# A two-block network: four modulation matrices of the second block move from the first mixer to the second, and are summed on VectorE there

## The chip, the cores and the metric

The kernel runs as one program on one core of a Trainium2 chip. The metric is the device time of a run in microseconds, the median of three runs. The core has five engines with an instruction stream each: TensorE (PE in the profile, with its weight loads as PEld), VectorE (DVE), ScalarE (ACT), GpSimd (POOL) and SyncE (SP), which here only issues DMAs. The streams meet in semaphores: an instruction adds to one, another stream waits until it has reached a number.

## What is computed

A sequence of 256 rows of 1024 features in fp32 goes through two transformer blocks. Each block takes a condition vector c and makes six modulation vectors of it, each of them the product of silu(c) with a matrix of 1024 x 1024 (4 MB):

```python
# first block: six parts mx[0..5], and mc[0..1] for 256 context rows
mx = split(silu(c) @ w_ada + b_ada, 6)
hx = rms_norm(x, g_pre_mix) * (1 + mx[1]) + mx[0]
x = x + mx[2] * rms_norm(token_mixer(hx, hc, ...), g_post_mix)      # mLSTM heads and a convolution
hx = rms_norm(x, g_pre_ffn) * (1 + mx[4]) + mx[3]
x = x + mx[5] * rms_norm(moe_ffn(hx, ...), g_post_ffn)              # 64 experts, top 8, one shared

# second block
shift1, scale1, gate1, shift2, scale2, gate2 = split(silu(c_2) @ w_ada_2 + b_ada_2, 6)
h = rms_norm(x, norm1_g) * (1 + scale1) + shift1
proj = h @ w_in                                                     # q, k, v, u, two branch gates
mixed = (g_attn * y_attn + g_pool * y_pool) @ w_out
x = x + gate1 * mixed
h2 = rms_norm(x, norm2_g) * (1 + scale2) + shift2
x = x + gate2 * hier_moe(h2, ...)                                   # 32 experts, top 2 of one group
return rms_norm(x, norm_f_g)
```

In the kernel's names the matrices are ada0 to ada5 for the first block and adb0 to adb5 for the second. adb0 and adb1 are shift1 and scale1; the four of the change are adb2 (gate1), adb3 (shift2), adb4 (scale2) and adb5 (gate2). None of these four is needed before the second mixer's end.

## The kernel before, in words

The work has four stages: first mixer (0 to about 256 us), first expert layer (to 754), second mixer (to about 965), second expert layer (to the end).

**Weights of the first mixer** come through three buffers of 4 MB, `BUF[0]` to `BUF[2]`, in the order of the list `STREAM` (name, buffer) at line 115. SyncE loads an item as soon as PE has counted the buffer's item before it as used (`stream_used`, in the order `USED`; `stream` at L543). After the sixteen items SyncE goes on with the pieces of the expert layer (1 MB each, `load_piece` at L603): those in `BUF[0]`, `BUF[1]` and `BUF[2]` wait for adb4, adb5 and w_out to be used up, those elsewhere for more. From the third group of experts on they also wait for `order_known`, which the routing gives.

**A modulation product** is `ada_parts` (L1055): silu(c) is the stationary side with 32 columns, the matrix the moving side of 512 columns; four products run side by side in the array and leave four partial sums for each vector in PS[5] and PS[6], which gather all vectors as rows. VectorE adds the bias (`ada_sum`, L1822) into `ada_rows`. Of these rows PE makes columns over the 128 partitions (`column_sums`, L1070) and, for the gates, one row spread over all partitions (`gate_rows`, L1076); `mixer_gate` (L2135) multiplies these with a gain.

**First mixer, PE from L1231.** For j = 0, 1, 2 the state products (L1240) are made, with the first sum over the convolution's channels (L1247) after j = 0 and adb0 and adb1 after j = 0 and 1. Then come the scores `qk` (L1257), the second sum of the convolution (L1262, for the variance) and the first two `seen_largest` (L1266, a product that spreads a row of maxima). Then the four heads' directions, gi = 0 to 3: one of adb2 to adb5, a wait for VectorE's last result (`hm_ready`), eight pairs of small products (L1287, L1288; called a head below), a further `seen_largest`. After that the output product (`mixed_out`, L1295) of the convolution's half, column sums (two banks of 30 columns) and gate rows, four transposes a block, the other half of the output product, and further gate rows between it and the transposes for the routing.

**VectorE beside it (L2018 to L2100)**: `states`, the convolution's mean and variance, `seen` (L2046), `convolution_normalised` (L2038) after the first score, and for each head the scaling and sum that read the four banks (L2071, L2075), a denominator and the normalised rows. **ScalarE** (L837 to L870) copies qk (L845), takes the root of the variance, the exponentials and, between the second and third of them, the four Silus of the convolution (L856); another kind of function than the last one costs a table load.

**Second mixer, PE from L1617**: transposes, then the projections in items of `ITEMS2` (q and k at L1627, v and u at L1637, the branch gates at L1667 in four pairs between the attention's heads), tables and pool products (L1643 to L1657), attention, the branch product (L1727), the output product (L1742), routing. SyncE loads the six items through `BUF[0]` and `BUF[1]` in turn (L660 to L675), then the second layer's expert pieces (L690 on).

## Time and profile before

| | |
|---|---|
| median of 3 runs | 1431.79 us (1428.27 to 1434.04) |
| profiled execution | 1431.23 us, its span 1429.5 us |
| mean granted clock of PE | 0.919 |
| busy: PE, DVE, ACT, POOL | 1177.6, 364.9, 181.8, 89.6 us |
| instructions | 21079 |
| HBM | 505.34 MB read, 354 GB/s over the span |

A timeline shows start and duration of instructions (one fp32 matrix product is two records, so "x32" are 16 products), and in brackets the idle time of the engine just before and what ended it. The chain that ended last is followed back from the last instruction to what released each step. The DMA share is the mean over the core's 16 DMA engines.

### The profile page before, as it was taken

Reading aid. Unit: us, or ns where it says so; the run is one execution under the profiler, and the core shown is the slowest. Engines: PE = TensorE matmul, PEld = TensorE weight load, DVE = VectorE, ACT = ScalarE, POOL = GpSimd, SP = SyncE. Lnnn points to the kernel's source line nnn. Section 1 sums busy time; section 2 is a strip of 40 time slices with the busy share of each in tenths; the row PEclk is TensorE's granted clock in tenths of the full one; section 3 lists DMA queues with packets and bytes.
Section 4 is the critical chain, followed back from the end, with each engine's and each line's share of the span. In section 5 each row is a group of like instructions: output and inputs, shape, how many; then the busy total and the mean of one; then the engine's idle time right before and its main releaser. Section 6 shows DMA issues by size and latency. Waiting matters only on the chain.

```text
span 1429.5 us, 21079 instructions
## 1 busy us (share of the span) xinstructions
PE 1177.6 (82%) x8938; PEld 607.4 (42%) x8938; DVE 364.9 (26%) x941; ACT 181.8 (13%) x370; POOL 89.6 (6%) x118
## 2 busy tenths in 40 slices
PE   5999989999999989999987999898475564655647
PEld 3663435655555545455546554344121221212212
DVE  1598755511111111111103054334010100100002
ACT  1210112411111111111113012012000000000000
POOL 2498000000000000000000000000000000000000
PEclk9999999999999999999998999999777886877878
DMA  9965993789999999999994222839999999999995
GB/s 388 344 262 236 422 420 146 304 321 388 419 420 420 420 420 420 420 420 420 420 429 191 118 118 118 368 130 382 428 428 428 426 428 429 427 429 425 430 424 222
DMA packets 51802, 507.81 MB, mean 355 GB/s; under 512 B 6445, under 2 KB 7637, under 8 KB 11001
## 3 DMA queue, kind: packets, MB, share of 16 engines
q1 hardware_dynamic: 49689, 503.07, 84.6%
q10 hardware_dynamic: 2016, 3.36, 0.7%
q8 instruction: 72, 1.18, 0.3%
q14 instruction: 25, 0.20, 0.0%
HBM read 505.34 MB, written 1.06 MB: 354 GB/s over the span
## 4 chain that ended last, share of the span: by engine, by line
PE 48%; DMA 26%; SPq 14%; DVE 7%; issue 3%; ACT 1%; POOL 1%; DVEq 0%; POOLq 0%; ACTq 0%
SPq L628 11%; DMA W<-in_w_expert_gate 6%; PE PS L1774 6%; PE PS L1598 5%; DMA W<-in_w_expert_up 4%; PE PS L1667 4%; PE PS L1608 3%; SPq L626 3%; PE PS L1788 3%; PE PS L1063 3%; PE PS L1464 3%; PE PS L1438 2%; DMA scr<-in_w_expert_up 2%; DMA W<-in_w_expert_down 2%; DMA hx<-in_w_expert_up 2%
## 5 line engine op out<-in xcount | busy, mean ns | idle before, releaser
L1774 PE MATMUL PS<-W,scr 128*32 128x512 f32 x640 | 143.6, 719 | 85.5 <-DMA W<-in_w_expert_gate 20.5
L1774 PE MATMUL PS<-scr 128*32 128x512 f32 x288 | 109.2, 724 | 62.7 <-DMA W<-in_w_expert_gate 31.8
L2299 DVE TENSOR_TENSOR scr<-scr,PS 128x256 f32<-128x256 f32 (+1 forms) x33 | 23.4, 710 | 518.3 <-PE PS L1774 262.9
L1598 PE MATMUL PS<-W,scr 128*32 128x256 f32 (+1 forms) x1936 | 136.4, 388 | 10.0 <-DMA W<-in_we_up 8.3
L1464 PE MATMUL PS<-scr 128*128 128x512 f32 x248 | 114.7, 605 | 0.0
L1598 PEld LDWEIGHTS PS<-W,scr 128*32 128x32 f32 (+1 forms) x1936 | 78.8, 116 | 67.4 <-issue 16.8
L1774 PEld LDWEIGHTS PS<-W,scr 128*32 128x32 f32 x640 | 34.7, 129 | 148.5 <-issue 103.3
L1438 PE MATMUL PS<-scr 128*128 128x128 bf16 x1536 | 91.8, 220 | 0.0
L908 ACT COPY scr<-PS 128x512 f32<-128x512 f32 x66 | 38.5, 585 | 410.1 <-PE PS L1438 407.4
L1438 PEld LDWEIGHTS PS<-scr 128*128 128x128 bf16 x1536 | 89.4, 98 | 1.0 <-issue 0.6
L1788 PE MATMUL PS<-W,scr 128*32 128x512 f32 x288 | 65.8, 678 | 16.4 <-DMA scr<-in_w_expert_down 7.6
L1464 PEld LDWEIGHTS PS<-scr 128*128 128x128 f32 x248 | 44.6, 189 | 60.1 <-issue 60.1
L1774 PEld LDWEIGHTS PS<-scr 128*32 128x32 f32 x288 | 25.1, 130 | 104.5 <-issue 70.9
L1788 PE MATMUL PS<-scr 128*32 128x512 f32 x176 | 57.0, 669 | 8.6 <-DMA W<-in_w_expert_down 7.6
L1598 PE MATMUL PS<-scr 128*32 128x256 f32 (+1 forms) x592 | 56.2, 387 | 6.8 <-DMA hx<-in_we_up 4.3
L1774 PE MATMUL PS<-hx,scr 128*32 128x512 f32 x96 | 56.8, 758 | 0.0
L1667 PE MATMUL PS<-W,hx 128*128 128x512 f32 x128 | 56.0, 595 | 0.0
L1608 PE MATMUL PS<-W,scr 128*32 128x512 f32 (+1 forms) x416 | 54.7, 596 | 0.0
L913 ACT ACTIVATE scr<-PS 128x256 f32<-128x256 f32 (+1 forms) x33 | 14.4, 435 | 300.4 <-PE PS L1774 226.6
L1063 PE MATMUL PS<-W,sc 128*32 128x512 f32 x384 | 48.0, 644 | 3.0 <-DMA W<-in_w_ada 2.9
L775 POOL TENSOR_SCALAR_AFFINE_SELECT W<-W 128x2048 f32<-128x2048 f32 x1 | 1.9, 1950 | 683.9 <-DVE W L2409 683.9
L770 POOL TENSOR_SCALAR scr<-scr,convw 128x256 f32<-128x256 f32 x44 | 44.5, 1010 | 4.3
(430 smaller groups left out, 1463.6 us busy)
## 6 DMA issues: line engine op xcount, KB each, us to landing
W<-in_we_up SPq DMA_DIRECT2D x46, 1024.0 KB, 24.6
W<-in_we_gate SPq DMA_DIRECT2D x45, 1024.0 KB, 24.4
W<-in_w_ada SPq DMA_DIRECT2D x10, 4096.0 KB, 15.0
W<-in_w_expert_gate SPq DMA_DIRECT2D x20, 2048.0 KB, 29.8
W<-in_w_expert_up SPq DMA_DIRECT2D x20, 2048.0 KB, 29.6
W<-in_we_down SPq DMA_DIRECT2D x38, 1024.0 KB, 24.6
W<-in_w_expert_down SPq DMA_DIRECT2D x16, 2048.0 KB, 32.3
scr<-in_w_expert_gate SPq DMA_DIRECT2D x10, 2048.0 KB, 26.9
```

The source lines that it names most:

```text
L626: expert = at if at < STATIC1 else sp.value_load(order[0:1, at:at + 1], min_val=1, max_val=E1) - 1
L628: sp.dma_start(piece_view(piece), src).then_inc(S[f"ring{SETS1.index(piece[0:2]) % 12}"], 16)
L770: step(g.tensor_scalar(tmp, upad[:, i, :, j:j + ROW], convw[:, 4 * j + i:4 * j + i + 1], None, ALU.mult))
L908: a.copy(hTe[:, 4 * q:4 * q + 4, :], PS[4 + q][:].rearrange("p (k s) -> p k s", k=4)).then_inc(S["x_hTe"], 1)
L1063: last = mm(PS[5 + h][32 * j:32 * j + 32, :], sc[:, 2 * j + kk, 30 - row:62 - row], ada_columns(n, 2 * j + kk, h), start=(row == 0 and kk ...
L1438: last = mm(PS[4 + k // 4][:, (k % 4) * P:(k % 4 + 1) * P], hs[:, part, b, k * P:(k + 1) * P], Sb[:, b, :], start=(q == 0), stop=(q == NB ...
L1464: last = mm(PS[2 * b + h][:, :], Ct[:, b * P:(b + 1) * P], Y[:, h * 512:(h + 1) * 512], start=False, stop=False)
L1598: m = mm(PS[4 + kind][at:at + size, 0:F1], hTe[:, k, at:at + size], piece_view((g, kind, j))[:, k, :], start=(k == 0), stop=(k == KD - 1))
L1608: m = mm(PS[6 + h][at:at + size, :], aT[:, c, at:at + size], piece_view((g, 2, j))[:, c, h * 512:(h + 1) * 512], start=(c == 0), stop=(c = ...
L1667: last = mm(PS[6 + n % 2][:, :], hT[:, k, b * P:(b + 1) * P], w2k[2 + half][:, k, h * 512:(h + 1) * 512], start=(k == 0), stop=(k == KD - 1))
L1774: m = mm(PS[4 + kind][j * CAP2:(j + 1) * CAP2, :], hTe[:, k, j * CAP2:(j + 1) * CAP2], piece_view2((g, kind, j))[:, k, :], start=(k == 0), ...
L1788: m = mm(PS[6 + h][j * CAP2:(j + 1) * CAP2, :], aT[:, c, j * CAP2:(j + 1) * CAP2], piece_view2((g, 2, j))[:, c, h * 512:(h + 1) * 512], st ...
```

## The change

1. `STREAM` ends with adb0, w_out, adb1; adb2 to adb5 are no longer in it. The buffers are dealt anew, w_out is loaded whole into `BUF[2]` (before, three of its eight parts lay in scratch), and the rows `post_mix` and `post_ffn` are loaded by SyncE ahead of in_qkv, into places of their own.
2. In the first mixer, PE's second sum of the convolution stands between the state products of j = 1 and adb1. The head loop has no modulation product; behind each head (`behind_head`) stand the next `seen_largest`, the gate rows and the column sums of the remaining vectors (18 columns, one bank). A head waits for `out_taken` (VectorE has read its banks) where it waited for `hm_ready`. VectorE takes the variance ahead of `states(2)`, normalises the convolution and adds the modulation's bias ahead of the heads, and makes the gates in the loop. ScalarE runs the Silus ahead of the copies of qk.
3. The four matrices come in the second mixer: SyncE's `late_modulation`, ahead of the third projection item, loads four bias tiles (128 x 1024, row 0 holding the bias) and 16 parts of 1 MB through three slots. VectorE adds each part with two fused multiply-adds of 1024 columns (`late_part`), in between its copies of q, k, v and u. PE sums over the partitions: the gates by a product with ones (four of 512 columns, behind the pool's first products), shift and scale by `late_columns`, 16 products with one moving column, after the attention. ScalarE copies the results (`second_gates` ahead of the exponentials of the attention).
4. The second block's normalised rows are transposed in the other order of features (`every_kd`), and w_in_2 and its gain are laid out to match; the products are the same in number and size.

```diff
-STREAM = [("ada0", 0), ("ada1", 1), ("in_conv", 2), ("in_og", 0), ("in_qkv", 1), ("ada2", 2), ("ada3", 0), ("ada4", 2), ("ada5", 0),
-          ("adb0", 2), ("adb1", 0), ("adb2", 1), ("adb3", 2), ("adb4", 0), ("adb5", 1), ("w_out", 2)]
-USED = ["ada0", "ada1", "in_conv", "in_og", "ada2", "ada3", "ada4", "ada5", "in_qkv",
-        "adb0", "adb1", "adb2", "adb3", "adb4", "adb5", "w_out"]
+STREAM = [("ada0", 2), ("ada1", 1), ("in_conv", 0), ("in_og", 2), ("in_qkv", 1), ("ada2", 0), ("ada3", 2), ("ada4", 0), ("ada5", 2),
+          ("adb0", 0), ("w_out", 2), ("adb1", 1)]
+USED = ["ada0", "ada1", "in_conv", "in_og", "ada2", "ada3", "ada4", "ada5", "in_qkv", "adb0", "adb1", "w_out"]
 AT = {n: i for i, n in enumerate(USED)}
-AHEAD = 5
+
+
+ADA_LATE = [("adb3", "shift"), ("adb4", "scale"), ("adb2", "gate"), ("adb5", "gate")]
+PARTS, PART_K, PART_SLOTS, PART_WORDS = 4, 2, 3, 2048
+FREE_RING = (8, 9, 10)
...
+            for name, src in (("post_mix", A["g_post_mix"][0]), ("post_ffn", A["g_post_ffn"][0])):
+                row(rowd[name], src)
             for n, _ in STREAM[4:]:
...
+                    sp.wait_ge(S["ada_summed"], 5)
+                    sp.wait_ge(S["gates_made"], 2)
...
+                    sp.wait_ge(S["stream_used"], AT[("adb0", "adb1", "w_out")[place // 4]] + 1)
...
+            def late_modulation():
+
+                sp.wait_ge(S["y_done"], 4)
+                for m, (n, _) in enumerate(ADA_LATE):
+                    sp.dma_start(late_sums[n], A["ada_bias_late"][m]).then_inc(S["ring4"], 16)
+                for i in range(len(ADA_LATE) * PARTS):
+                    if i >= PART_SLOTS:
+                        sp.wait_ge(S["part_used"], i - PART_SLOTS + 1)
+                    sp.dma_start(part_slots[i % PART_SLOTS], A["w_ada_late"][i // PARTS, i % PARTS])\
+                        .then_inc(S[f"ring{FREE_RING[i % PART_SLOTS]}"], 16)
+
             for n, i in AT2.items():
+                if i == 2:
+                    late_modulation()
...
+            sp.wait_ge(S["ada_summed"], 10)
             fill((5, 4, 6, 7))
...
+            act.wait_ge(S["norm_ms"], 3)
+            step(a.activation(crstd, crstd, ACT.Sqrt), S["norm_root"])
+            act.wait_ge(S["cn_ready"], 1)
+            for i in range(4):
+                step(a.activation(mixT[:, 4 + i, :], ctmp[:, i, :], ACT.Silu, scale=cols[:, C_LNG + i:C_LNG + i + 1],
+                                  bias=cols[:, C_LNB + i:C_LNB + i + 1]), S["mixT_conv"], wait=False)
             act.wait_ge(S["qk_mm"], 2)
             for r in range(2):
                 step(a.copy(qk.rearrange("p c (q r) t -> p c q r t", r=2)[:, :, :, r, :],
                             PS[r][:].rearrange("p (c q t) -> p c q t", c=2, q=2)), S["qk_ready"], wait=False)
 
-            act.wait_ge(S["norm_ms"], 3)
-            step(a.activation(crstd, crstd, ACT.Sqrt), S["norm_root"])
             for gi in range(4):
                 act.wait_ge(S["exp_in"], gi + 5)
                 step(a.activation(dts[gi % 2], dts[gi % 2], ACT.Exp, scale=-1.0), S["exp_out"])
-                if gi == 1:
-                    for i in range(4):
-                        act.wait_ge(S["cn_ready"], 1)
-                        step(a.activation(mixT[:, 4 + i, :], ctmp[:, i, :], ACT.Silu, scale=cols[:, C_LNG + i:C_LNG + i + 1],
-                                          bias=cols[:, C_LNB + i:C_LNB + i + 1]), S["mixT_conv"], wait=False)
-
+
+            act.wait_ge(S["ada_summed"], 5)
+            for n, (i, b, s) in enumerate(((4, 1, 0), (1, 0, 2))):
+                mod_columns(5, i, b, s, n == 1)
+            root_table()
...
+            def second_gates():
+
+                for n in range(4):
+                    act.wait_ge(S["ada_summed"], 6 + n)
+                    step(a.copy(gate2[:, n // 2, n % 2 * 512:n % 2 * 512 + 512], PS[n][:]), S["ada_ready"], wait=False)
...
+            act.wait_ge(S["ada_summed"], 10)
+            step(a.copy(modc[:, 1, 2:4, :, 2], PS[3][:, 384:400].rearrange("p (m k) -> p m k", m=2)), S["ada_ready"], wait=False)
...
+                elif j == 1:
+                    pe.wait_ge(S["csq_ready"], 1)
+                    conv_sum(7)
                 if j < 2:
...
-            for gi, n in enumerate(("adb2", "adb3", "adb4", "adb5")):
+            def behind_head(gi):
+
+                if gi < 2:
+                    seen_largest(gi + 2)
+                if gi == 0:
+                    pe.wait_ge(S["ada_rows_ready"], 3)
+                    pe.wait_ge(S["gate_sel"], 2)
+                    gate_rows(0, (5, 6))
+                elif gi == 1:
+                    pe.wait_ge(S["gates_made"], 1)
+                    gate_rows(1, (5, 6))
+                elif gi == 2:
+                    pe.wait_ge(S["gates_made"], 2)
+                    column_sums(5, N_ADA1, every_kd(ada_rows)).then_inc(S["ada_summed"], 1)
+
+            for gi in range(4):
                 c, d = gi // 2, gi % 2
-                ada_parts(n)
                 pe.wait_ge(S["sT_ready"], gi + 1)
                 if gi:
-                    pe.wait_ge(S["hm_ready"], gi)
+                    pe.wait_ge(S["out_taken"], gi)
                 else:
 
                     pe.wait_ge(S["norm_ms"], 3)
@@ -1288,8 +1323,7 @@
                     last = mm(PS[(3, 7)[h % 2]][:, hp * 129:hp * 129 + 129], qT[half, hp, c * P:(c + 1) * P],
                               state[half, 0 if c == d else 1, d, hp, :], start=True, stop=True)
                 last.then_inc(S["out_mm"], 1)
-                if gi < 2:
-                    seen_largest(gi + 2)
+                behind_head(gi)
...
-            pe.wait_ge(S["ada_rows_ready"], 3)
-            column_sums(4, 30, ada_rows.rearrange("t (k p) -> t k p", k=KD))
-            column_sums(7, 30, every_kd(ada_rows)).then_inc(S["ada_summed"], 1)
-            pe.wait_ge(S["gate_sel"], 4)
-            gate_rows(0, (5, 6))
...
+            for n in range(4):
+                if n % 2 == 0:
+                    pe.wait_ge(S["ada_rows_ready"], 3 + (3, 4)[n // 2])
+                mm(PS[n][:, :], ones[:], gate2[:, n // 2, n % 2 * 512:n % 2 * 512 + 512], start=True, stop=True).then_inc(S["ada_summed"], 1)
...
+            pe.wait_ge(S["ada_ready"], 7)
+
+            def late_columns():
+
+                for m, n in enumerate(("adb3", "adb4")):
+                    for k in range(KD):
+                        at = 384 + KD * m + k
+                        last = mm(PS[3][:, at:at + 1], every_kd(late_sums[n])[:, k, :], ones[:, 0:1], start=True, stop=True, skip_group_check=True)
+                last.then_inc(S["ada_summed"], 1)
...
+            late_columns()
 
 
             loaded2(4)
             pe.wait_ge(S["attn_done"], 1)
...
-            states(2)
             dve.wait_ge(S["conv_sum_mm"], 2)
             step(v.tensor_scalar(crstd, PS[7][:, 0:T], 1.0 / CONV_C, EPS, ALU.mult, ALU.add), S["norm_ms"])
+            states(2)
...
+            def scored(gi):
+
+                dve.wait_ge(S["exp_out"], gi + 5)
+                dve.wait_ge(S["qk_ready"], 2)
+                step(v.tensor_tensor(dts[gi % 2], dts[gi % 2], qk[:, gi // 2, :, :], ALU.mult), S["sT_ready"])
+
+            convolution_normalised()
+            dve.wait_ge(S["stream_used"], AT["adb1"] + 1)
+            for h in range(2):
+                ada_sum(1, h, S["ada_rows_ready"] if h else None)
             dve.wait_ge(S["exp_out"], 4)
             seen(0)
+            seen(1)
+            scored(0)
+            scored(1)
             for gi in range(4):
...
+                    step(v.tensor_tensor(rows, rows, nd[:, :, 0:DV], ALU.add))
+                if gi < 2:
+                    scored(gi + 2)
+                    mixer_gate(gi, 3 + gi)
...
+            def late_part(i):
+
+                n = ADA_LATE[i // PARTS][0]
+                if i == 0:
+                    dve.wait_ge(S["ring4"], 16 * RING_USES[4] + 16 * len(ADA_LATE))
+                ring = FREE_RING[i % PART_SLOTS]
+                dve.wait_ge(S[f"ring{ring}"], 16 * RING_USES[ring] + 16 * (i // PART_SLOTS + 1))
+                for k in range(PART_K):
+                    kk = i % PARTS * PART_K + k
+                    step(v.scalar_tensor_tensor(out=late_sums[n], in0=part_slots[i % PART_SLOTS][:, k * D:(k + 1) * D], scalar=sc[:, kk, 32:33],
+                                                in1=late_sums[n], op0=ALU.mult, op1=ALU.add), S["part_used"] if k == PART_K - 1 else None)
+                if i % PARTS == PARTS - 1:
+                    dve.sem_inc(S["ada_rows_ready"], 1)
+
+            parts_before = (6, 9, 12, 15)
             for q in range(4):
+                for i in range(parts_before[q - 1] if q else 0, parts_before[q]):
+                    late_part(i)
                 dve.wait_ge(S["in2_mm"], q + 1) if q < 3 else dve.wait_ge(S["stream2_used"], 1)
                 dst = (qT2 if q < 2 else kT2)[:, 2 * (q % 2):2 * (q % 2) + 2, :]
                 step(v.tensor_copy(dst, PS[4 + q][:].rearrange("p (m t) -> p m t", m=2)), S["in2_ready"])
+            late_part(len(ADA_LATE) * PARTS - 1)
```

## Rows read from the trace of the kernel before

**Rows 1.** The page, share of each of 40 slices of 35.7 us: granted clock, DMA.

```profile
PEclk9999999999999999999998999999777886877878
...
DMA  9965993789999999999994222839999999999995
```

**Rows 2.** Timeline of PE, end of the first expert layer (start, duration, engine, line, what).

```profile
743.95 5.20 PE L1608 MATMUL PS<-scr 128*32 128x512 f32 x32 [2.41 <-DMA scr<-in_we_down]
```

**Rows 3.** Timeline of PE, first mixer from 160 to 252 us.

```profile
161.46 3.64 PE L1063 MATMUL PS<-W,sc 128*32 128x512 f32 x32
...
167.71 1.99 PE L1262 MATMUL PS<-scr,ones 128*128 128x256 f32 x8
...
174.92 0.49 PE L1287 MATMUL PS<-scr 128*128 128x129 f32 x2
...
178.26 1.12 PE L1268 MATMUL PS<-hx,ones 128*128 128x512 f32 x2
...
198.52 6.55 PE L1063 MATMUL PS<-W,sc 128*32 128x512 f32 x32 [2.10 <-DMA W<-in_w_ada]
...
247.38 3.60 PE L1079 MATMUL PS<-scr 128*128 128x512 f32 x8
```

**Rows 4.** Chain that ended last, first mixer (start, duration, piece).

```profile
208.41 13.93 PE PS L1300 x32
...
222.34 5.53 PE PS L1073 x32
...
227.87 3.58 PE PS L1079 x4
```

**Rows 5.** The load of adb2 issued at 153.1 us, and its time to landing.

```profile
L554 SPq DMA_DIRECT2D W<-in_w_ada x1: 327/327/327, 153.1 to 153.1; - x1
...
DMA to landing us min/median/max: 16.2/16.2/16.2
```

**Rows 6.** Timeline of DVE, first mixer.

```profile
168.12 0.43 DVE L2023 TENSOR_TENSOR scr<-scr 128x258 f32<-128x258 f32 x1
...
172.34 1.12 DVE L2052 SCALAR_TENSOR_TENSOR scr<-PS,small,scr 128x128 f32<-128x128 f32 x4
...
173.38 0.68 DVE L1925 TENSOR_TENSOR hx<-ident,small 128x512 f32<-128x512 f32 x1
...
174.69 1.75 DVE L2041 RECIPROCAL scr<-scr 128x256 f32<-128x256 f32 x1
...
176.48 1.22 DVE L2042 TENSOR_TENSOR scr<-scr 128x1024 f32<-128x1024 f32 x1
...
187.09 1.13 DVE L2071 TENSOR_SCALAR scr<-PS,small 128x129 f32<-128x129 f32 x4 [3.58 <-PE PS L1288]
...
188.25 0.89 DVE L2075 TENSOR_TENSOR scr<-scr,PS 128x129 f32<-128x129 f32 x4
```

**Rows 7.** Timeline of ACT, first mixer.

```profile
168.18 1.07 ACT L845 COPY hx<-PS 128x512 f32<-128x512 f32 x2 [25.96 <-PE PS L1257]
...
177.78 1.28 ACT L856 ACT_TABLE_LOAD   x1 [3.30 <-DVE scr L2042]
...
179.08 2.07 ACT L856 ACTIVATE scr<-scr,cols 128x256 f32<-128x256 f32 x4
```

**Rows 8.** Windows, first mixer: busy time of each engine, granted clock, DMA share, GB/s.

```profile
198.00:204.00 6.00, 5.48 (x28) 1.39 (x32) 2.47 (x8) 0.00 (x0) 0.00 (x0) 0.50 0.96 406
...
225.00:231.00 6.00, 6.00 (x16) 4.07 (x17) 0.00 (x0) 0.40 (x3) 0.00 (x0) 0.50 0.14 59
```

**Rows 9.** Chain, second expert layer: one matrix product with one moving column.

```profile
986.04 0.22 PE PS L1422 x2
```

**Rows 10.** Timeline of DVE: its last work before the second mixer's projections.

```profile
764.83 1.90 DVE L2184 TENSOR_SCALAR hx<-PS,am,modc 128x256 f32<-128x256 f32 x4 [0.65 <-PE PS L1330]
```

**Rows 11.** DVE line 2161, all of its instructions (ns minimum, median, maximum).

```profile
L2161 DVE SCALAR_TENSOR_TENSOR x<-hx,small,x x8: 750/752/752, 242.9 to 760.3; 128x512 f32<-128x512 f32 x8
```

**Rows 12.** The 1 MB load of x on an empty queue, to landing.

```profile
DMA to landing us min/median/max: 5.5/5.5/5.5
```

112 lines of the change are left out of this document (41 added, 71 removed).

## The prediction

> **What bounds the kernel now.** I read the slices of the page first. The DMA row [rows 1] is full in slices 9 to 20, the first expert layer, and from slice 27 on, the second one. It reads 2, 2, 2, 8, 3 in slices 22 to 26 (786 to 965 us), the second mixer, so 16.8 MB of weights find room there. In the first mixer (up to about 256 us) it is full only from 140 to 222 us, while four of the matrices in question arrive. Both expert layers end with the loads: the last down product of the first one still stands 2.41 us for its weights [rows 2]. But the loads of a layer start from events of the mixer before it (w_out used up, the routing known, the places of the ring free again). So each layer is shifted as a whole by what its mixer gains or loses, and the question is how long the two mixers' chains are.
>
> The timeline of PE in the first mixer comes next [rows 3]. From 153 to 208 us PE alternates between a modulation product (3.6 us a matrix, 16 products of which four run side by side) and a head (eight pairs of rows, 3.4 us). The products fill the time in which VectorE normalises the head before. Behind the heads the chain of waits has the first half of the output product, the column sums and a gate row [rows 4], and the second half ends where the next gate rows start, at 247.4 us [rows 3].
>
> **What goes.** Four products of 3.6 us, with the loads they stand for (the one at 198.52 took 6.55 us instead of 3.6: PE had stood 2.1 us for its load, and the granted clock was 0.50) [rows 3, 8]. Between the two halves of the output product 5.53 of column sums and 3.58 of gate row go [rows 4]. The gate rows and copies behind 247.4 run beside VectorE and ScalarE, which set the end there: I count them at nothing.
>
> **What the new order costs until head 0.** adb1 is now the third in the load queue, behind adb0 and the whole of w_out, as adb2 was behind adb0 and adb1. adb2's load, issued at 153.1, landed 16.2 us later [rows 5], at 169.3; issue and bytes ahead of it are the same for adb1 now. PE is through with the state products of j=1 at 161.5, where adb1's product began before, and with the moved sum for the convolution (1.92 more) at 163.45 [rows 3]. It stands 5.9 us.
> Then, at full clock: adb1's product 3.6 (172.9); state products and six VectorE steps of 0.46, as before 3.5 from the first product's start (176.4) [rows 6]; reciprocal 1.75 and product 1.22 (179.5) [rows 6]; ScalarE now runs the four Silus before the copies of qk, table load 1.28, Silu 2.07, copies 1.07 (184.0) [rows 7]; the first maximum 0.86 (184.9) [rows 3]; VectorE twice 1.12 and 0.68 before the first score, then 0.69 (189.2) [rows 6]; head 0, 3.36 (192.5). Before, head 0 ended at 178.3 [rows 3]: 14.2 us later.
>
> **The heads.** With the products gone they form a circle. After head 0: scaling 1.13 and sum 0.89 free the banks [rows 6], but PE has a maximum (some 0.9) and a gate row (1.79, half of the 3.60 for two) to do [rows 3], so head 1 ends 6.0 later. From then VectorE leads: per head 2.05 for the banks, 1.1 for the next `seen`, 0.6 for the denominator, 0.7 to 1.4 for the rows, 0.7 for the score and 1.4 for the gate, together 6.6 and 7.3; head 2 ends 6.3 after head 1, and head 3, which waits for the second gate and eight column sums (2.2, at 0.24 to 0.28 each), 7.5 after head 2, at 212.2 [rows 6]. That is 19.8 us for three heads where 30.1 stood (178.3 to 208.4).
> Output product 13.9, transposes and copies 2.0, output product 13.9 [rows 3, 4]: 242.1 us against 247.4, a gain of 5.3 at full clock.
>
> **The clock.** All this holds at full clock, and that is the doubt. After a stand of 2.1 us the granted clock was 0.50 from 198 to 204; in the column sums, with PE busy throughout but with 30 moving columns, it was 0.50 from 225 to 231 [rows 8]. The new order stands 5.9 us before adb1 and 8.4 us between qk and the first maximum, and has a third weak stretch from head 2 to the column sums. I charge: adb1's product 2.1 (between 0 and the 3.0 of the row 6.55 against 3.6); the maximum, head 0 and the gate row behind it 5.0 (0 to 6.0, all of them doubled); column sums, head 3 and the start of the output product 5.0 (0 to 6.5). Together 12.1, bounds 0 and 15.5. So the first mixer ends 6.8 us later than before; bounds 5.3 earlier and 10.2 later.
> The Trainium skill (TensorE: Matmul & The Clock Gate, Part 1) says that for modelling, the ramp penalty of a typical kernel is under 1% of its span, and advises against fitting it. Taken as leave to drop the term it gives the sum of the first rival below; taken as a ceiling, 14.3 us here, it leaves my charge standing. The row at 0.50 clock, 3.0 us lost on one product, speaks for charging each such stretch.
>
> **The second mixer.** The loads: 2.1 MB of bias rows and 16.8 MB of parts, from the end of the first expert layer, behind the projection weights that are still arriving; at 0.42 MB per us 45 us, in a stretch where the DMA row reads 2. VectorE: 32 fused multiply-adds on 1024 columns. The trace has 512 columns at 0.752 us [rows 11] and none at 1024; twice that is the upper bound (1.50), the lower is the 1.22 of a plain product of that width [rows 6]; I take 1.32 with its gap, as part of the 0.752 is fixed. A part takes 2.64, sixteen 42. A slot turns around in 2.64, some 0.5 of issue and at most the 5.5 us of a 1 MB load on an empty queue [rows 12]: 8.6 over three slots, 2.9 a part; the loads alone need 2.5. VectorE is free at 766.7 [rows 10]; bias rows and first part, 3.1 MB or 7.4 us, come behind what is still arriving then, so the start is about 773. From there sixteen parts at 2.7 to 2.9 with four copies of 0.7, partly in the gaps, end at 819 to 822. PE wants these copies at 821.8, after 56 us of projections that need nothing of VectorE. I charge 0.5; bounds 0, and 8 if a part takes 3.5. Up to 3.2 a part the projection weights issued behind the late loads also come in time. If this cover went, each 0.1 us a part would cost 1.6.
> PE gets four products of ones with the gate sums, 3.5 (3.60 for four such [rows 3]), right in its chain: nothing else could run, since the scores wait for the ScalarE copies. It gets 16 products with one moving column, 0.22 each [rows 9] (upper bound 0.28, from the 5.53 for 16 of 30 columns less its slow part [rows 4]): 3.5, of which 0.7 lie in the wait for VectorE's last copy there: 2.9, bounds 2.0 and 4.0. They are as narrow as the column sums that brought the clock down [rows 8]: 0.9 for a fall into the next product, bounds 0 and 3.0. The ScalarE copies run beside PE, and SyncE's new wait delays the expert loads by 3 us at a time when the queue later stands empty (slice 26 reads 3, rows 1): nothing. Sum 7.8, bounds 5.5 to 18.5.
>
> **Sum.** 1431.2 (the profiled execution, span 1429.5; the median of the three is 1431.8, so no correction) plus 6.8 plus 7.8 is 1445.8 us.
>
> **Rivals.**
> 1. The clock holds. Not slower then: minus 5.3 and plus 6.9, 1432.8 us; with one fall of the three 1435 to 1438. It decides from the point at which PE's clock stays at 1.00 through the two stands ahead of head 0. Against it stands the fall after 2.1 us [rows 8]; for it only that the falls before were few. Chance 0.22 (1429 to 1438).
> 2. The load of adb1 arrives in time, so that PE doesn't stand there, because the queue drains sooner than it did for adb2: 5.9 and the 2.1 of the first fall go. With the other falls 1438; with a full clock 1427, and with the gate sums and column products of the second mixer hidden in waits besides, 1420. For it speaks only that adb0 and w_out have most of their bytes through when adb1 is issued; against it the landing in [rows 5], with the same bytes ahead. Chance of ending under 1424.6: 0.09.
> 3. The parts run at 3.5 us or more: VectorE comes 8 us late to the copies and the third projection's weights are late too: 1454, up to 1460. For it: three slots leave no reserve, and bias rows come first; against it an almost empty queue. Chance 0.15.
> The forecast itself has 0.54, with a range of its own from 1439 to 1452.
>
> **How the numbers follow.** Half a per cent (7 us) is what a measurement of this kernel tells from no change. Slower than 1439: the forecast and the third rival, 0.69; same: the first rival and the upper part of the second, 0.22; faster 0.09. The range leaves out the second rival's best case and the third's worst: 1429 to 1456. The time is that of the forecast, 1446.
>
> **What would show it.** PE standing from about 163 to 169 for adb1's load; PE standing some 8 us before the first maximum, with the Silus ahead of the copies on ScalarE; a granted clock of 0.50 there and around head 3; heads 6 to 8 us apart; the last output product ending near 254 (242 would be the first rival). In the second mixer, the sixteenth part done by 822 plus the shift, 32 steps near 1.3 us, 3.5 us between the pool products and the scores, and the column products near 3.5. The first expert layer's length (283 to 754) unchanged would confirm that it only shifts; if it became shorter by more than 5 us, the argument of the first part is wrong.

## The result, and the profile after

The changed kernel takes 1461.2 us (median of four runs, 1458.3 to 1464.2) against 1432.2 for the kernel before: a ratio of 1.0206, 95% interval 1.0177 to 1.0236. The forecast was 1446, range 1429 to 1456: the side was right, the size (14 us) was half of what came (29), and the time lies outside the range.

The page of the changed kernel, first the span, then the two lines that stand in [rows 1] (40 slices, now of 36.5 us):

```profile
span 1459.8 us, 20925 instructions
...
PEclk9999868899999999999998999999777878778878
DMA  9955910679999999999999932827999999999995
```

The granted clock now dips in slices 4 to 7 as well (counted from 0; 146 to 292 us), and the DMA row is as full in both expert layers as it was. So the two mixers are to be read. Timeline of PE in the first mixer of the changed kernel:

```profile
170.03 6.62 PE L1082 MATMUL PS<-W,sc 128*32 128x512 f32 x32 [7.12 <-DMA W<-in_w_ada]
...
187.59 3.78 PE L1289 MATMUL PS<-hx,ones 128*128 128x512 f32 x4 [8.27 <-ACT hx L878]
193.81 0.80 PE L1322 MATMUL PS<-scr 128*128 128x129 f32 x2 [2.44 <-DVE scr L2105]
...
214.94 3.99 PE L1092 MATMUL PS<-small,scr 128*128 128x18 f32 x16 [1.56 <-DVE scr L2086]
218.77 0.78 PE L1322 MATMUL PS<-scr 128*128 128x129 f32 x2
...
241.78 14.00 PE L1334 MATMUL PS<-W,scr 128*128 128x512 f32 x32 [1.01 <-DVE scr L2152]
...
262.89 1.97 PE L1357 MATMUL PS<-ident,hx 128*128 128x128 f32 x8 [4.31 <-DVE hx L2214]
264.66 6.93 PE L1393 MATMUL PS<-scr,hx 128*128 128x64 f32 x32
271.38 3.62 PE L1398 MATMUL PS<-ident,hx 128*128 128x128 f32 x16
274.79 3.73 PE L1579 MATMUL PS<-W,hx 128*128 128x512 f32 x8
```

PE stands 7.12 us for adb1 and 8.27 before the first maximum (5.9 and 8.4 were forecast), and adb1's product (6.62 instead of 3.64), the maxima and head 0 run at half clock; so do the column sums and head 3 (granted clock 0.50 from 214 to 226 us). The second half of the output product ends at 255.6 us, where [rows 3] have 247.4: 8.2 later. Then comes what the forecast did not have: PE stands 4.31 us, and the turn (the transposes of a block) behind this stand, the routing product and its transposes run at half clock. Two more views: the same stretch in the kernel before, where a gate row lies between the two turns, and the granted clock of that stretch in the changed kernel (window, length, busy PE, PEld, DVE, ACT, POOL, clock, DMA share, GB/s):

```profile
251.70 1.88 PE L1079 MATMUL PS<-scr 128*128 128x512 f32 x4
...
255.89 3.76 PE L1373 MATMUL PS<-scr,hx 128*128 128x64 f32 x32
...
261.23 1.02 PE L1559 MATMUL PS<-W,hx 128*128 128x512 f32 x2
```

```profile
262.00:275.00 13.00, 12.11 (x57) 12.11 (x58) 5.59 (x20) 5.24 (x9) 0.00 (x0) 0.50 0.99 414
```

The first product of the first expert layer starts at 274.8 instead of 261.2: 13.6 later, 5.3 of them behind the output product.

A trace is one execution, and how far the clock falls differs between executions. Six of the kernels below leave the first mixer as it is up to the output product. In them and in the changed kernel adb1's product takes 5.0 to 6.6 us, and the second half of the output product starts 4.3 to 8.2 us later than in the kernel before; this trace has the latest start of the seven.

Timelines of the second mixer of the changed kernel, PE and then DVE:

```profile
835.45 3.67 PE L1662 MATMUL PS<-scr,flip 128*128 128x512 f32 x8 [0.78 <-DVE scr L2461]
841.83 5.30 PE L1671 MATMUL PS<-W,scr 128*128 128x256 f32 x16 [2.70 <-DVE W L2468]
846.96 3.60 PE L1676 MATMUL PS<-scr,ones 128*128 128x512 f32 x8
...
853.13 0.49 PE L1715 MATMUL PS<-scr 64*128 64x128 f32 x4 [0.84 <-DVE scr L2474]
...
919.61 7.77 PE L1703 MATMUL PS<-ones,W 128*128 128x1 f32 x32
927.24 29.29 PE L1762 MATMUL PS<-W,scr 128*128 128x512 f32 x64
```

```profile
790.42 2.60 DVE L2450 SCALAR_TENSOR_TENSOR W<-scr,sc,W 128x1024 f32<-128x1024 f32 x2 [10.87 <-DMA scr<-in_w_ada_late]
...
835.34 2.60 DVE L2450 SCALAR_TENSOR_TENSOR scr<-scr,sc 128x1024 f32<-128x1024 f32 x2
838.09 2.87 DVE L2465 COPY scr<-PS 128x512 f32<-128x512 f32 x4
840.99 2.87 DVE L2468 COPY W<-PS 128x512 f32<-128x512 f32 x4
```

The last of the late parts ends at 837.9, and the copies of v and u and of the pair bias queue behind it. PE stands 2.70 us for them and begins the pool products at half clock (0.50 from 842 to 844 us). In three of the kernels below these products take 3.69 us behind the same stand, so this fall of the clock does not come every time. The scores start 21.7 us later than before, where the turns that open the second mixer start 12.8 later (774.95 against 762.13). The column products take 7.6 us, 0.8 of which fill a wait, and the branch product behind them 29.29 us where it took 27.70. The second expert layer starts 30.1 us later (1008.76 against 978.65), and that is the whole difference of the spans (30.3).

The terms, forecast and measured, in us of later end:

| term | forecast | measured |
|---|---|---|
| first mixer to the end of the output product | 6.8 | 8.2 |
| from there to the first expert product | 0 | 5.3 |
| first expert layer | 0 | -0.7 |
| late parts, copies queued behind them | 0.5 | 5.5 |
| gate sums | 3.5 | 3.4 |
| column products | 2.9 | 6.8 |
| clock behind them | 0.9 | 1.6 |
| sum | 14.6 | 30.1 |

### The profile page after: what moved, and what is told of

It reads as the page before. It is cut to its first block, busy times and chain, and to the rows that moved or that the text cites. A ratio compares the mean times of both kernels' runs of the same rounds, so it can differ in the third digit from the quotient of the medians.

```text
span 1459.8 us, 20925 instructions
## 1 busy us (share of the span) xinstructions
PE 1188.9 (81%) x8826; PEld 620.8 (43%) x8826; DVE 405.6 (28%) x971; ACT 181.2 (12%) x370; POOL 89.6 (6%) x118
## 4 chain that ended last, share of the span: by engine, by line
PE 38%; DMA 26%; SPq 14%; DVE 6%; issue 2%; ACT 1%; DVEq 0%; ACTq 0%
SPq L637 11%; DMA W<-in_w_expert_gate 6%; PE PS L1809 6%; PE PS L1617 5%; DMA W<-in_w_expert_up 4%; PE PS L1690 4%; PE PS L1823 3%; PE PS L1627 3%; SPq L635 3%; PE PS L1484 2%; PE PS L1458 2%; DMA scr<-in_w_ada_late 2%; DMA W<-in_w_expert_down 2%; DMA scr<-in_w_expert_up 2%; DMA hx<-in_w_expert_down 2%
## 5 line engine op out<-in xcount | busy, mean ns | idle before, releaser
L931 ACT ACTIVATE scr<-PS 128x256 f32<-128x256 f32 (+1 forms) x33 | 14.4, 435 | 294.9 <-PE PS L1809 221.9
L1617 PEld LDWEIGHTS PS<-scr 128*32 128x32 f32 (+1 forms) x592 | 31.5, 117 | 29.5 <-issue 9.2
## 6 DMA issues: line engine op xcount, KB each, us to landing
W<-in_w_ada SPq DMA_DIRECT2D x6, 4096.0 KB, 14.2
```

The costliest lines, as they stand in the source:

```text
L1617: m = mm(PS[4 + kind][at:at + size, 0:F1], hTe[:, k, at:at + size], piece_view((g, kind, j))[:, k, :], start=(k == 0), stop=(k == KD - 1))
```

## The experiments

Twelve kernels were run; each was timed beside the kernel before. Unless another base is named, the edit is made on the changed kernel. The kernel before was at 1429.7 to 1431.8 us beside these runs, so it is the ratios that are to be compared, with 1.0206 (1.0177 to 1.0236) for the changed kernel. Of the nine single edits only adb1 first lies clearly under that, and the column products cut into four nearly so; the intervals of the other seven overlap with it, and what they show is read from their traces. The first four asked where the clock and the order of loads cost.

**Filling products behind the output product.**

```diff
             mixed_out(0, range(NB))
+            dense(2, 5)        # products of ones, 128x512, into an unused bank
...
             turn_rows(0, 0)
+            dense(4, 6)
             turn_rows(0, 1)
```

> The changed kernel with six dense products that nobody reads (ones by ones, 128x512) in the places where the removed gate rows stood: two behind the second half of the output product, four between the two blocks' transposes. In the changed kernel PE stands from 255.7 to 262.9 us but for 1.2 us, and then runs the routing product and 16 transposes at a granted clock of 0.50 (6.7 and 3.4 us, where the kernel before took 3.8 and 1.8). Theory A (the removed gate rows were what kept PE's clock up): the transposes and the routing product run at 1.00, the shared expert's first product starts 5 us earlier, the whole run is 5 us shorter, about 1456. Rival B (the routing product is slow for another reason, such as the layout of w_router or contention): no change of either, 1461 or 1 to 2 us more if the dense products are in the way.

Measured: 1457.4, ratio 1.019 (1.0165 to 1.0216). Timeline of PE:

```profile
262.19 3.76 PE L1400 MATMUL PS<-scr,hx 128*128 128x64 f32 x32
...
267.54 1.02 PE L1586 MATMUL PS<-W,hx 128*128 128x512 f32 x2
```

From the end of the output product to the first expert product it is 13.9 us instead of 19.2: the whole 5.3 come back with products that compute nothing. This does not vary between executions: from the start of that half of the output product it is 33.0 us in all nine traces of the changed kernel and its variants that lack this filling, and 27.7 to 27.8 in the three that have it and in the kernel before (28.4 in the control below). The gate rows that were taken away had been that filling.

**Filling products before adb1 and before the maxima.** Eight `dense` products before the wait for adb1, nine before the first maximum.

> The changed kernel with dense products that nobody reads in the two stands ahead of head 0: eight (6.9 us) before adb1's product, where PE stands 7.1 us for the load, and nine (7.8 us) before the first maximum, where it stands 8.3 us for VectorE and ScalarE. Nothing is moved or removed. Theory A (the clock costs 13 us of the first mixer: 3 at adb1, 1.7 at the maxima, 3.3 at head 0, 3 at the products behind it, more later): adb1's product takes 3.6 instead of 6.6 us and head 0 3.4 instead of 5.8, the output product's second half ends 8 to 12 us earlier than at 255.7, total about 1451. Rival B (the stands themselves, that is the load and the chain through VectorE and ScalarE, are what costs; the half clock is hidden under it): the end moves by less than 3 us, total 1458 to 1461.

Measured: 1459.4, ratio 1.0205 (1.0177 to 1.0233): by the time alone it can't be told from the changed kernel. By the trace adb1's product takes 3.64 and the maxima 1.98; head 0, behind its own stand of 3.29 us, is again at half clock:

```profile
170.14 3.64 PE L1082 MATMUL PS<-W,sc 128*32 128x512 f32 x32
...
190.73 0.80 PE L1330 MATMUL PS<-scr 64*128 64x129 f32 x2
```

Warming one weak stretch does not carry to the next. From the start of adb1's product to the second half of the output product it is 68.4 us, against 68.7 to 71.8 in the seven traces with this stretch as it was: 0.3 to 3.4 us gained, where theory A has 8 to 12. Rival B is the nearer one, and the 4.8 us that adb1's product and the maxima lose at half clock are in part hidden under waits. The time of the whole run can't price this filling either: at the end of the first expert layer PE stands 3.47 us here, for nothing that the profile shows, and the second mixer opens 2.3 us later than in the changed kernel.

**adb1 loaded ahead of w_out.**

```diff
-           ("adb0", 0), ("w_out", 2), ("adb1", 1)]
+           ("adb0", 0), ("adb1", 2), ("w_out", 1)]
```

> The changed kernel with adb1 loaded ahead of w_out (adb1 in buffer 2, w_out in buffer 1, the expert pieces' waits to match). adb1 should land near 160, before PE needs it at 163. Theory A (the late load starts the trouble: 7.1 us of stand, 3 us of half clock in its product): PE doesn't stand there, head 0 begins 9 to 10 us earlier, and the mixer ends 9 us earlier or somewhat more: about 1451. Rival B (VectorE and ScalarE are then the limit, since their chain before head 0 has its own length): head 0 moves by less than 5 us. Rival C (the expert pieces now wait longer, as four of them stand behind w_out): the mixer is 9 us shorter but the first expert layer gives part back, 1455.

Measured: 1451.2, ratio 1.0145 (1.0121 to 1.017).

```profile
162.56 3.64 PE L1082 MATMUL PS<-W,sc 128*32 128x512 f32 x32
...
177.15 3.78 PE L1289 MATMUL PS<-hx,ones 128*128 128x512 f32 x4 [8.27 <-ACT hx L878]
...
230.95 14.00 PE L1334 MATMUL PS<-W,scr 128*128 128x512 f32 x32 [1.01 <-DVE scr L2152]
```

No stand, no half clock at adb1, and the output product ends 10.8 us sooner than in the changed kernel's trace (6.9 to 10.8 against the seven). The second mixer opens 8.7 us sooner (766.25) and the second expert layer 10.9 (997.90): the first expert layer passes on most of the gain, and the second mixer is 2.2 us shorter in this trace. The stand and its clock are the largest single piece of the loss, and the output product never waited for w_out, in this order or the other.

**The column products spread between the heads' branch products**, in groups of four.

> The changed kernel with the 16 one-column products spread over the attention (4, 4, 4, 3 between dense products, one at the end) instead of all behind it. There they took 7.7 us at half clock, and the branch product behind them 29.2 instead of 27.7. Theory A (in a block of narrow products the granted clock falls, and this doubles them and slows the next product): spread they cost 3.5 in all and the branch product 27.7, so 5 us less, 1456. Rival B (a one-column product behind a full weight load costs 0.48 at any clock): they cost 7.7 as before, the sum is unchanged, 1461.

Measured: 1463.2, ratio 1.0222 (1.0199 to 1.0246): no gain. Timeline of PE (eight instructions are four products), and the windows of two groups:

```profile
862.97 1.83 PE L1702 MATMUL PS<-ones,W 128*128 128x1 f32 x8
...
887.95 2.06 PE L1702 MATMUL PS<-ones,W 128*128 128x1 f32 x8
```

```profile
862.90:864.60 1.70, 1.70 (x9) 1.63 (x7) 0.69 (x1) 0.00 (x0) 0.00 (x0) 1.00 0.00 0
...
887.90:889.80 1.90, 1.90 (x11) 1.86 (x9) 0.54 (x2) 0.00 (x0) 0.00 (x0) 1.00 1.01 276
```

At a granted clock of 1.00, with a busy and with an empty queue, each instruction still takes 0.21 to 0.24 us. So the clock was not the price of the columns. The clock did cost something behind the block: the branch product is back at 27.70, but the transposes behind the second group take 1.34 us instead of 0.88. (The execution with the profile, 1468.7 us, is 5.5 above the median.)

The next four took up one piece each, and then all.

**The last late part behind the copies of the pair bias.**

```diff
-            late_part(len(ADA_LATE) * PARTS - 1)
             for n in range(4):          # copies of v and u
...
             for q in range(4):          # copies of the pair bias
...
+            late_part(len(ADA_LATE) * PARTS - 1)
```

> The last of the sixteen late parts (two fused steps, 2.60 us) is put behind the four copies of the pair bias, so that the copies of v and u and of the pair bias no longer queue behind it on VectorE. Theory A (the parts ended too late: TensorE stood 2.70 us in front of the pool products and those ran at half clock, 5.30 us instead of 3.7): the stand goes, the pool products take 3.7 and the scores start 4.0 to 4.7 us sooner after the end of the first expert layer; 1461.2 becomes 1457. Rival B (the copies are late for another reason, or the gate sums now wait for the part that was moved): under 1 us moves, 1461.

Measured: 1459.6, ratio 1.0201 (1.0184 to 1.0218).

```profile
835.47 5.37 PE L1662 MATMUL PS<-scr,flip 128*128 128x512 f32 x8 [2.28 <-DVE scr L2461]
840.67 3.62 PE L1671 MATMUL PS<-W,scr 128*128 128x256 f32 x16
```

The stand of 2.70 is gone and the pool products are fast. But VectorE, not PE, sets the start at 835.4: PE had its projections done 1.5 us sooner in this run, waited 2.28 us for a copy behind the parts, and the half clock is in the product before. From the opening turns to the scores it is 76.1 us, against 78.2 in the changed kernel; but adb1 first, which leaves this stretch alone, has 76.1 as well. So no gain is shown, where theory A has 4.0 to 4.7. VectorE reached its copies no sooner, since the fifteen parts before them ended where they had.

**The Silus behind the exponentials of heads 0 and 1.**

```diff
-            act.wait_ge(S["cn_ready"], 1)
-            for i in range(4): ... ACT.Silu ...
             act.wait_ge(S["qk_mm"], 2)
             for r in range(2): ... copy of qk ...
             for gi in range(4):
+                if gi == 2: (the wait and the four Silus)
                 act.wait_ge(S["exp_in"], gi + 5)
```

> ScalarE copies qk first and runs the exponentials of heads 0 and 1 before the four Silus of the convolution, which come ahead of the exponential of head 2. Theory A (the Silus, with the wait for the convolution's normalisation and their table load, hold the copies back: they start at 186.49, while qk was there at 179.3 and the states at 180.1): TensorE's maxima start near 181 instead of 187.6; VectorE, busy until 184.9 with the convolution, then has the first score 4.9 us sooner, and head 0 starts near 189 instead of 193.8. With a shorter stand before the maxima they may also keep the full clock (a further 1 to 3). 1461.2 becomes 1456 (1453 to 1457). Rival B (VectorE or the tables take it back: Silus ahead of head 2 are late, two more table loads): under 1 us, 1461.

Measured: 1456.5, ratio 1.0176 (1.0159 to 1.0193).

```profile
179.98 1.98 PE L1290 MATMUL PS<-hx,ones 128*128 128x512 f32 x4 [1.22 <-ACT hx L874]
...
188.35 0.80 PE L1323 MATMUL PS<-scr 128*128 128x129 f32 x2 [6.39 <-DVE scr L2106]
```

The stand before the maxima falls from 8.27 to 1.22 and the maxima keep the full clock, but the stand before head 0 grows from 2.44 to 6.39, for VectorE. From the end of adb1's product to the second half of the output product it is 60.5 us, against 63.8 to 65.2 in the seven traces: 3.3 to 4.7 us gained (4.9 forecast).

**The gate sums in PE's stands behind the branch product.** Two before the transposes of the mixed rows, two behind them, with the banks and the counts of the waits to match.

> The four products of ones with the summed gate rows (3.6 us before the scores) are moved into the two stands of TensorE behind the branch product (2.36 and 1.65 us in the trace of after). Theory A (they cost their own length where they stand, since nothing runs beside them, and are free in a stand): the scores come 3.5 us sooner, the second expert layer 3 us sooner; 1461.2 becomes 1458. Rival B (the gate sums kept the clock up ahead of the scores, or the copies of the gates are late for the last output product): scores at half clock or a new wait, within 1 us of 1461.

Measured: 1458.4, ratio 1.0188 (1.0171 to 1.0205).

```profile
954.08 1.88 PE L1697 MATMUL PS<-scr,ones 128*128 128x512 f32 x4
956.61 1.96 PE L1772 MATMUL PS<-ident,hx 128*128 128x128 f32 x16 [0.65 <-DVEq L2548]
```

Two sums now fill a stand that falls from 2.36 to 0.65. From the opening turns the scores come 3.3 us sooner, the second expert layer 1.5. That the run gains is likely, but the ratio does not show it.

**All of it together**: adb1 first, the filling behind the output product and around the maxima, two filling products before the column sums, and the last three edits.

> All that has been found, at once: adb1 loaded ahead of w_out, products of ones as filling around the maxima, the column sums and the turns of the first mixer, the Silus behind the exponentials of heads 0 and 1, the last late part behind the pair bias, the gate sums in the stands of the second mixer. If each charge is a separate link of one chain they add up: 1461.2 less 10.0 (adb1 first), 5.2 (turns and routing at full clock), 4.9 (Silus), 4.3 (last part), 3.5 (gate sums), and up to 5 for head 0, column sums and head 3 at full clock: 1433, down to 1428, against 1430 for the kernel before. What is left then is the column products (7.0 and 1.6). Rival: the gains overlap (VectorE leads the heads whatever TensorE's clock, and the second mixer waits for its loads): 1440 or more.

Measured: 1443.3, ratio 1.0081 (1.0064 to 1.0097), as the rival had it (1440 or more). The first mixer gave what was forecast: the first expert product starts at 253.8, 21.0 us sooner. The rest did not:

```profile
751.66 1.81 PE L1579 MATMUL PS<-ones,zeros 128*128 128x512 bf16 x4 [3.59 <-issue]
...
830.97 3.75 PE L1687 MATMUL PS<-scr 128*128 128x256 f32 x8 [3.26 <-DVE scr L2487]
```

At the end of the first expert layer 6.6 us are gone (the opening turns come 14.4 sooner), 3.6 of them in a stand that the profile puts down to nothing. And with the gate sums away, the part put behind the pair bias (4.17 us there, 2.60 elsewhere) holds back the pool copies: a new stand of 3.26, and half clock behind it. Two of the edits were in each other's way.

The last four went after the price of the columns.

**Column products cut into four.**

```diff
-   last = mm(PS[3][:, at:at + 1], every_kd(late_sums[n])[:, k, :], ones[:, 0:1], ...)
+   for j in range(4):
+       last = mm(PS[3][32 * j:32 * j + 32, at:at + 1],
+                 every_kd(late_sums[n])[:, k, 32 * j:32 * j + 32], ones[:, 0:1], ...)
```

> Each of the sixteen column products of the second mixer (weights 128 by 128, one moving column, 32 instructions, 7.77 us in the trace of after) is cut into four with 32 columns of weights each, which land in the four quarters of the same PSUM column: 64 products, 128 instructions. Theory A (what a column product costs is the loading of its 128 columns of weights, 0.24 us an instruction at either clock, not the one moving column, and four narrow ones load side by side): the trace of after has 16 instructions of that form (line 1435, 128 by 32 weights, one column) in 0.33 us, 0.02 each, so 128 take 2.6 us: 5 us less, 1461.2 becomes 1456. Rival B (the price is one per instruction): 128 instructions of 0.06 us or more, 7.8 us or longer, 1461 or up to 1470.

Measured: 1453.1, ratio 1.0155 (1.013 to 1.018).

```profile
915.67 2.16 PE L1704 MATMUL PS<-ones,W 128*32 128x1 f32 x128
917.76 27.73 PE L1764 MATMUL PS<-W,scr 128*128 128x512 f32 x64
```

Four times the instructions in 2.1 us instead of 7.6, and in this trace the branch product keeps its clock: 5.5 and 1.6 back. Rival B is out.

**Neighbouring columns as weights.** The columns of the two matrices and their bias lie in another order in memory; the products keep their form.

```diff
-   every_kd(late_sums[n])[:, k, :]
+   late_sums[n][:, k * P:(k + 1) * P]
```

> The sixteen late column products keep their form (weights 128 by 128, one moving column, 32 instructions), but the columns of the two matrices and of their bias lie in another order in memory, so that each product's weights are 128 neighbouring columns of the sum instead of every eighth. In the traces, at a granted clock of 1.00 in both, loading 128 by 128 weights took 0.335 us in every late column product (and in the column sums whose weights are every eighth column) and 0.192 us where the weights are neighbours (first half of the column sums of the kernel before; line 1422, from which the prediction took its price). Theory A (the price is the stride of the weights): 0.135 us an instruction at full clock, 4.3 us in all, 3.3 less than in after, and up to 1.6 less in the branch product if the shorter stretch keeps the clock; 1461.2 becomes 1457. Rival B (it is one moving column, or the conflict with the loads that run then): 7.6 us as before, 1461.

Measured: 1458.3, ratio 1.0198 (1.018 to 1.0217). All weight loads of that line in the changed kernel, then in this one (ns minimum, median, maximum):

```profile
L1703 PEld LDWEIGHTS PS<-ones,W x32: 312/335/336, 919.6 to 927.0; 128*128 128x128 f32 x32
```

```profile
L1708 PEld LDWEIGHTS PS<-ones,W x32: 187/192/193, 918.5 to 921.9; 128*128 128x128 f32 x32
```

3.6 us instead of 7.6 (4.3 forecast). The stride of the weights was half of the price. The branch product is still slow (29.41): the stretch is shorter, but the clock falls all the same.

**The second version with everything**: to "all of it together" come the cut columns, the column sums of the first mixer cut in the same way, two filling products ahead of head 0, and the last three late parts behind the first soft maximum.

> The kernel with all changes together, and four more: the late column products and the column sums of the first mixer cut into four with 32 columns of weights each, two more filling products ahead of head 0, and the last three late parts (only the last gate sum needs them) behind the first soft maximum of the second mixer. Expected against 1443.3: late columns 5 less, no stand of 3.3 before the pool products' second half, 1 to 2 less at half clock there and behind the columns, 1 to 2 in the first mixer: 1431 (1427 to 1435), against 1430.8 for the kernel before. Rival: the parts that were moved hold VectorE back between the heads, or the gate sum waits for them: 1438 or more.

Measured: 1422.3, ratio 0.9931 (0.9915 to 0.9947): faster than the kernel before by 0.7%.

```profile
197.55 1.19 PE L1094 MATMUL PS<-small,scr 128*32 128x18 f32 x64
...
247.98 3.60 PE L1592 MATMUL PS<-W,hx 128*128 128x512 f32 x8
...
819.02 0.49 PE L1731 MATMUL PS<-scr 64*128 64x128 f32 x4 [0.84 <-DVE scr L2493]
```

The first expert product starts 13.3 us sooner than in the kernel before, the scores 12.4 sooner (831.42 there). The cut column products take 2.1 us again, but the branch product behind them takes 29.43: the clock falls into it here (0.51 from 888.3 to 891.8 us), so the cut alone does not keep it.

**The control: the kernel before, with its column sums cut and nothing else.**

> A control on the kernel before, whose modulation is unchanged: only its column sums (32 instructions with 30 moving columns and weights of 128 by 128, 5.53 us between the halves of the output product, and two groups of 16 with 6 columns at the start) are cut into four with 32 columns of weights each. It tells how much of what the best version gains over the kernel before is due to the late matrices and how much to the cut. Theory A (the price is the weights' width, and the fall of the clock to 0.50 from 225 to 231 us comes with it): the sums take about 2.2 us, the gate row and the turns behind them run at full clock (2 less): 1431.8 becomes 1426 to 1427, so that the best version (1422.3) is still ahead. Rival B (the sums are as long as before, or something else ends the first mixer): 1431.

Measured: 1423.9, ratio 0.9954 (0.9939 to 0.997).

```profile
195.31 3.64 PE L1063 MATMUL PS<-W,sc 128*32 128x512 f32 x32 [0.20 <-DMA W<-in_w_ada]
...
216.66 1.79 PE L1074 MATMUL PS<-small,scr 128*32 128x30 f32 x128
218.38 1.98 PE L1080 MATMUL PS<-scr 128*128 128x512 f32 x4
...
250.68 3.60 PE L1560 MATMUL PS<-W,hx 128*128 128x512 f32 x8
```

The sums take 1.7 us where the chain of [rows 4] has 5.53, the gate row behind them no longer falls to half clock, and the first expert product starts 10.6 us sooner, more than these two make. By the traces 3.1 us come before 154 us, where two groups of sums take 0.44 each instead of 1.03 and 0.95 and the product between them keeps its clock (10.60 instead of 12.28), and 2.5 around the load that PE stood for in [rows 3] (0.20 left of 2.10). One trace of each kernel can't tell how much of this is the edit's. The interval overlaps that of the version with everything: moving the four matrices cannot be shown to be worth anything. By the traces it is worth 2.7 us in the first mixer (13.3 less 10.6) and costs 2.9 in the second up to its output product (the opening turns are 12.3 sooner than in the kernel before, 749.79 against 762.13, the output product of the second mixer 9.4, 923.00 against 932.39) and 4.1 up to the second expert layer. The control reaches that layer 0.6 us later than the version with everything (971.02 against 970.40), although PE stood 3.25 us at the end of its first expert layer, for nothing that the profile shows. So the move has no lead that could be called its own. The control was given only the cut of the sums; what filling products would do to it was not run.

## Why the prediction was wrong, point by point

**What bounds the kernel, and how a shift travels.** Right. Loads of a layer start from the mixer before it. From its first product to the turns of the second mixer it is 499.9 to 502.3 us in eleven traces, whatever the first mixer gained or lost. In the other three, with the unexplained stand at its end, it is 503.9 to 506.7; the first kernel with all edits lost 6.6 us there.

**The stand for adb1.** Right: 7.12 us against 5.9. The load issued at 152.5 us landed 17.4 us later, 1.2 more than that of adb2 in [rows 5]. That ScalarE would run the Silus first was right too, and 8.27 us of stand (8.4 forecast) shows it.

**Heads in a circle of VectorE.** Right: head 1 ends 7.8 us behind head 0 (the work between them at half clock; 6.0 forecast), head 2 another 6.0 (6.3).

**The clock in the first mixer.** Right as a mechanism, in each of the three places, and near in size: end of the output product 8.2 late, and 4.3 to 8.2 over seven traces, with 6.8 forecast. One part of it is no matter of the clock: the eight column sums, forecast at 2.2 us, take 3.8 (214.94 to 218.77), for the reason given below for the late columns. The first rival (the clock holds) is refuted, and the second (adb1 in time) by the stand.

**"The gate rows and copies behind 247.4 run beside VectorE and ScalarE, which set the end there: I count them at nothing."** This step failed, for 5.3 us. They did lie beside other work, so their going freed nothing; but they had kept PE busy through the waits, and with them the clock. The filling products show it: 5.3 us back. I had named the clock's price where PE would newly stand (before adb1, before the maxima) and did not ask it where work goes and the wait stays.

**"VectorE is free at 766.7 [rows 10]; bias rows and first part, 3.1 MB or 7.4 us, come behind what is still arriving then, so the start is about 773."** This step failed, and with it the overlap: it had the late parts done before PE wants the copies. Sixteen parts of 2.6 us are as forecast (2.64), and VectorE stood only 2.2 us in all for a later part. But the first began at 790.4, which is 777.6 in the time of the kernel before: the issue of four bias loads takes 2.9 us on SP, and the first part landed 20.1 us after its issue. So the last ended at 825.1, not 819 to 822, and the four copies of v and u and four of the pair bias, which I did not count as queued behind the part, came on top. Forecast 0.5, measured 5.5, of which 1.7 are the pool products' clock. It is the third rival's effect (8 us) by another cause: a late start, not slow parts.

**Gate sums.** Right, 3.4.

**"16 products with one moving column, 0.22 each."** This step failed, for 3.9 us. The price is from [rows 9], a product whose weights are neighbouring columns: two instructions, 0.22 us together. The late columns take every eighth column of the sum as weights, and a product takes 0.48. The kernel before shows both: the weight loads of its column sums (line 1073) change from one length to the other within a few products, at a granted clock of 1.00 in both groups. Windows 223.0 to 223.8 and 224.4 to 224.8 of that line:

```profile
L1073 PEld LDWEIGHTS PS<-small,scr x9: 192/192/192, 222.9 to 223.7; 128*128 128x128 f32 x9
...
L1073 PEld LDWEIGHTS PS<-small,scr x4: 334/336/337, 224.1 to 224.8; 128*128 128x128 f32 x4
```

The first group reads neighbours, the second `every_kd(ada_rows)`. I took the second for the clock ("less its slow part") and cut it from the bound; it was there before the clock fell. With the weights as neighbours the sixteen products took 3.6 us, the price that I had put. The Trainium skill (Advanced Engine Details and Errata, Memory Cachelines) says that reads of SBUF lose speed when each element falls in another line of 16 bytes. Every eighth float does; the 0.335 against 0.192 us agrees.

**The clock behind the columns.** 1.6 measured, 0.9 forecast: right as a mechanism, and within its bounds.

The three steps that failed make 14.2 of the 15.5 us missed, all on one side. The second mixer's sum, 17.3 us, still lies inside its bounds (5.5 to 18.5); the first mixer, 13.6 us up to the first expert product, is over its upper bound of 10.2, for the term that stood at nothing and had no bound. The range ended at 1456, and left out the third rival's worst (1460), which the kernel reached.

## What to carry to other kernels

Work that lies beside a wait is not free to remove on TensorE: look at what the granted clock does when it goes, and price the next products at half clock. Take a product's price from a row with the same layout of weights, not only the same shape; where many narrow products must be made, cut the weights into quarters that land in different output partitions. And before a move is judged by the best version of it, give the version without the move the same repairs: here one of them, the cut of the sums, closed it.

## What the runs showed of the hardware

- Weights of 128 by 128 floats load in 0.192 us where they are neighbours and in 0.335 where they are every eighth column, at a granted clock of 1.00 in both. A one-column product then follows every 0.11 and every 0.24 us. Cut to 128 by 32, strided as well, the loads took 0.160 us but followed each other every 0.016 (128 of them in 2.1 us).
- PE can be busy without a gap and the clock still falls: in the 7.6 us of column products it went from 1.00 to 0.50 at about 924, and in those of 3.6 us it still fell into the branch product. With the same sums in 2.1 us it fell in one kernel (the second version with everything, branch product 29.43 us) and not in the other (27.73). The same code behind the same stand of 2.70 us ran at half clock in some traces (pool products 5.30 to 5.38 us in three) and not in others (3.69 in three).
- Half clock costs more than it seems from one row. Against full clock in the two mixers of the changed kernel, in durations: adb1's product 3.0, maxima 1.8, heads 0 and 3 each 2.5, maximum and gate row behind head 0 1.8, output product 1.3, turn, routing and transposes 5.7, pool products 1.7, branch product 1.6. That is 22 us, or 1.5% of the span, in durations; what was hidden under waits did not lengthen the run. The Trainium skill (TensorE: Matmul & The Clock Gate, Part 1) says that for modelling the ramp penalty is under 1% of a typical span. It says so of the ramp, and the trace shows that the later falls, counted together, can be more.
- At the end of the first expert layer PE stood 3.25 to 3.59 us in three of the fourteen traces ("issue" in the profile: filling before adb1 and the maxima, all of it together, the control) and not at all in the others. Nothing here tells why, and it stays open.
